# A Mixture-of-Experts layer on one core: how the weights of late expert blocks are loaded, and in which order those blocks run

## The reference

```python
lg = hf @ w_rg + b_rg                     # 8 groups
grp = argmax(lg)                          # top-1 group of a token
le_sel = (hf @ w_re + b_re) of that group # 8 experts in it
top_v, top_j = top_k(le_sel, 2)           # top-2 experts: 1024 choices, 64 experts
wts = softmax(lg)[grp] * softmax(top_v)
# each choice: (silu(x @ w_g[e]) * (x @ w_u[e])) @ w_d[e], weighted and added to its token
out = rmsnorm(x + sum of the two choices)
```

## Time and profile before

| | |
|---|---|
| time, median of 3 runs | 1350.87 us (1350.43 to 1354.53) |
| the profiled execution's own time | 1351.41 us |
| its span, first to last instruction | 1349.6 us |
| PE busy | 1156.8 us (86%) |
| DVE, ACT, POOL busy | 355.5, 234.3, 227.6 us |
| bytes moved by DMA | 435.80 MB, mean 323 GB/s |
| mean granted TensorE clock | 0.967 of full speed |
| chain that ended last | DMA 50%, PE 41%, DVE 4%, ACT 3% |

### The profile page before, as it was taken

How to read it: one execution, slowest core, us unless ns; L and a number is a source line. 1 busy time by engine, 2 the same in 40 slices (tenths; PEclk the granted TensorE clock), 3 DMA queues, 4 the chain that set the end, 5 groups by cost and what they waited for, 6 DMA issues and landing times.

```text
span 1349.6 us, 15238 instructions
## 1 busy us (share of the span) xinstructions
PE 1156.8 (86%) x5137; PEld 564.9 (42%) x5137; DVE 355.5 (26%) x700; ACT 234.3 (17%) x496; POOL 227.6 (17%) x271
## 2 busy tenths in 40 slices
PE   6999999999999999999888878777887778777881
PEld 5788777688843333333222222222222222222220
DVE  3899334444454222222000000000000000000004
ACT  4232324663100000000100000000001000010002
POOL 3455444083001000010010010000100010000100
PEclk9999999999999999999999999999999999999996
DMA  6431311314369999999999999999999999999974
GB/s 215 128 116 63 125 63 63 133 54 187 123 255 372 403 412 419 419 414 420 401 426 425 422 423 426 424 423 424 426 424 418 424 422 418 421 417 425 425 324 191
DMA packets 58516, 435.80 MB, mean 323 GB/s; under 512 B 10528, under 2 KB 10685, under 8 KB 26234
## 3 DMA queue, kind: packets, MB, share of 16 engines
q1 hardware_dynamic: 53034, 430.10, 77.4%
q0 software_dynamic: 5312, 5.28, 1.2%
q10 hardware_dynamic: 144, 0.07, 0.0%
HBM read 429.10 MB, written 18.36 MB: 332 GB/s over the span
## 4 chain that ended last, share of the span: by engine, by line
DMA 50%; PE 41%; DVE 4%; ACT 3%; issue 2%; SPq 1%; POOL 0%; POOLq 0%; DVEq 0%; ACTq 0%
DMA sb_weights<-in_w_exp_up 49%; PE ps_proj L1417 12%; PE ps_proj L1682 9%; PE ps_proj L1647 4%; PE ps_scores L1702 4%; PE ps_proj L1468 2%; PE ps_proj L1595 1%; PE ps_proj L1599 1%; PE ps_proj L1592 1%; PE ps_proj L1547 1%; PE ps_proj L1550 1%; PE ps_proj L1553 1%; DVE sb_x L1366 1%; PE ps_scores L1482 1%; PE ps_aT L1691 1%
## 5 line engine op out<-in xcount | busy, mean ns | idle before, releaser
L1682 PE MATMUL ps_proj<-sb_weights,sb_scratch 128*64 128x512 f32 x1984 | 471.7, 628 | 73.3 <-DMA sb_weights<-in_w_exp_up 71.9
L1682 PEld LDWEIGHTS ps_proj<-sb_weights,sb_scratch 128*64 128x64 f32 x1984 | 166.3, 144 | 371.8 <-issue 370.7
L1702 PE MATMUL ps_scores<-sb_weights,sb_scratch 128*64 128x512 f32 x992 | 228.5, 597 | 21.8 <-ACT sb_scratch L904 21.8
L1306 DVE TENSOR_TENSOR sb_scratch<-sb_scratch,ps_proj 128x256 f32<-128x256 f32 x62 | 26.1, 421 | 641.1 <-ACT sb_scratch L902 641.1
L659 POOL TENSOR_TENSOR sb_tick<-sb_tick 1x1 f32<-1x1 f32 x62 | 11.4, 184 | 882.5 <-ACT sb_scratch L909 783.4
L1702 PEld LDWEIGHTS ps_scores<-sb_weights,sb_scratch 128*64 128x64 f32 x992 | 67.0, 136 | 145.6 <-issue 109.5
L1417 PE MATMUL ps_proj<-sb_hT_r,sb_ring_r 128*128 128x512 f32 x512 | 124.0, 394 | 0.0
L902 ACT ACTIVATE sb_scratch<-ps_proj 128x256 f32<-128x256 f32 x62 | 23.8, 384 | 529.2 <-PE ps_proj L1682 529.2
L1417 PEld LDWEIGHTS ps_proj<-sb_hT_r,sb_ring_r 128*128 128x128 f32 x512 | 94.8, 188 | 26.9 <-issue 6.5
L604 POOL TENSOR_TENSOR sb_ring_r<-sb_ring,sb_ring_r 128x1024 fp32r<-128x1024 f32 x32 | 76.2, 2394 | 65.6 <-ACT sb_ring_r L721 64.6
L909 ACT ACTIVATE sb_scratch<-ps_scores 128x512 f32 (+1 forms) x62 | 37.0, 597 | 268.2 <-PE ps_scores L1702 268.2
(11 more groups left out here) (281 smaller groups left out, 872.1 us busy)
## 6 DMA issues: line engine op xcount, KB each, us to landing
sb_weights<-in_w_exp_up SPq DMA_DIRECT2D x62, 2048.0 KB, 14.9
sb_weights<-in_w_exp_down SPq DMA_DIRECT2D x62, 2048.0 KB, 10.5
sb_weights<-in_w_exp_gate SPq DMA_DIRECT2D x62, 2048.0 KB, 22.1
sb_ring<-in_w_in SPq DMA_DIRECT2D x9, 2048.0 KB, 9.0
sb_x<-in_x SPq DMA_DIRECT2D x8, 512.0 KB, 5.1
sb_dense<-expert_rows SPq DMA_DIRECT2D x4, 1024.0 KB, 7.9
sb_ring<-in_w_conv_pw SPq DMA_DIRECT2D x1, 2048.0 KB, 9.1
sb_ring<-in_w_attn_up SPq DMA_DIRECT2D x1, 2048.0 KB, 7.8
```

The source lines that it names most:

```text
L1306: dve.tensor_tensor(act, gsig, ps_gu[:, 256:512], ALU.mult).then_inc(act_ready, 1)
L1682: last = mm(ps_gu[g * BLK:(g + 1) * BLK, :].rearrange("p (a n) -> p a n", a=2), hTb[:, c, half * BLK:(half + 1) * BLK], weights[:, slice(6 ...
L1702: last = mm(ps_y[g * BLK:(g + 1) * BLK, :], actT[:, j, half * BLK:(half + 1) * BLK], weights[:, place(parity, 4 + half), 2 * j + g, :], st ...
```

## The change

Blocks 0 to 17 stay as they are: their weights are loaded one set for each block, in the order of the experts (`MINLOOP = 16` table places and the two first blocks). For the blocks behind them, the late ones:

- Late blocks of even experts take the even positions, in rising order of the expert; late blocks of odd experts take the odd positions, in falling order. A position is i, and its block is i + 2. Since even positions use the even weight set, all late blocks of one expert meet the same set, one after the other with a block of the other class between them.
- If one class has fewer blocks than the other, positions of that class at the end have no block; they run all the same, on rows that are scattered nowhere. The number of positions is 16 + 2 x the larger class.
- SP first runs its old loop for 16 places, then a second loop over loads: for load n it reads its position from `load_pos` and the expert from `expert_at`. A position whose expert was the expert of the position two before it has no load.
- PE reads for each late block from `load_at` how many loads must have landed: it waits for 16 * (loads + 1), where it waited for 16 * b.
- DVE reads for each late block from `nat_at` which place of the old order it is, and with that the offset and the row numbers: three reads of a register where one was.
- The tables are computed by DVE and PE: `late_turns` (eight instructions on at most 64 x 128 elements) and two instructions in `sorted_starts` (DVE), `turn_starts` and `turn_rows` (PE) in block 1, `list_turns` (DVE, eleven with its signal) behind `take_slots`, `load_row` (PE) and `list_loads` (DVE) ahead of block 16. Five new constants widen the table of constants from 1445 to 1881 columns of 512 bytes.
- ACT, POOL and PE wait for `turns_listed` in place of `listed`, and the special case of an odd count is gone.

With the reference's counts the late positions 16 to 59 hold, on the even side, experts 20, 22, 24, 26, 28, 30, 32, 34, 36, 38, 40, 42, 46, 48, 50, 52, 54, 56, 58, 60, 60, 62 (22 blocks), and on the odd side 63, 61, 61, 59, 59, 57, 55, 53, 51, 49, 47, 45, 43, 41, 39, 37, 35, 33, 27, 23, 21, 19 (22 blocks). So blocks 23, 27 and 58 have the expert of the block two before them.

The core of the diff:

```diff
 @@ SyncE
-            nblk = sp.value_load(count_i[0:1, 0:1], min_val=MINLOOP, max_val=MAXB - AHEAD)
-            with sp.Fori(0, nblk) as i:
-                e = sp.value_load(small_i[0:1, bass.ds(i, 1)], min_val=0, max_val=NE - 1)
+            def load_expert_weights(n, e, pos):
                 for third in range(3):
                     if third == 0:
-                        sp.wait_ge(gu_used, 2 * i + 2)
+                        sp.wait_ge(gu_used, 2 * pos + 2)
                     if third == 2:
-                        sp.wait_ge(down_used, i + 1)
-                    sp.wait_ge(in_w[third], 16 * i + 16)
+                        sp.wait_ge(down_used, pos + 1)
+                    sp.wait_ge(in_w[third], 16 * n + 16)
...
-                    load_third(i + AHEAD, third, bass.ds(e, 1), in_w)
+                    load_third(pos + AHEAD, third, bass.ds(e, 1), in_w)
+            with sp.Fori(0, MINLOOP) as i:
+                load_expert_weights(i, sp.value_load(small_i[0:1, bass.ds(i, 1)], min_val=0, max_val=NE - 1), i)
+            sp.wait_ge(turns_listed, 1)
...
+            sp.wait_ge(loads_listed, 1)
+            with sp.Fori(0, loads) as n:
+                pos = sp.value_load(load_pos[0:1, bass.ds(n, 1)], min_val=MINLOOP, max_val=MAXPOS - AHEAD)
+                e = sp.value_load(expert_at[0:1, bass.ds(pos, 1)], min_val=0, max_val=NE - 1)
+                load_expert_weights(n + MINLOOP, e, pos)
 @@ VectorE, in sorted_starts
+                link(dve.tensor_scalar(late_lo, efirst, float(MINLOOP), None, ALU.max))
+                dve.tensor_scalar(late_n, eend, float(MINLOOP), late_lo, ALU.max, ALU.subtract).then_inc(late_in, 1)
+            def late_turns():
+                dve.wait_ge(late_done, 1)
+                link(dve.tensor_copy(turn_lo, ps_oT[0:NE, 336:337]))
+                link(dve.tensor_tensor(turn_hi, turn_lo, late_n, ALU.add))
...
+                dve.tensor_scalar(late_b, ones_e, late_n, 1.0, ALU.mult, ALU.min).then_inc(loads_in, 1)
+            def list_turns():
+                dve.wait_ge(loads_done, 1)
...
+                dve.engine_nop().then_inc(turns_listed, 1)
+            def list_loads():
+                dve.wait_ge(loads_done, 2)
+                dve.tensor_scalar(load_pos[0:1, :], ps_oT[0:1, 344:344 + P], npos_f[0:1, :], None, ALU.min).then_inc(loads_listed, 1)
 @@ VectorE, late blocks
                 gate_and_up(i + AHEAD)
-                sorted_to_block(dve.value_load(start_i[0:1, 1:][:, bass.ds(i, 1)], min_val=0, max_val=2 * SEQ * KD))
-                list_rows(i + AHEAD, slots[:, AHEAD:][:, bass.ds(i, 1)])
+                nat = dve.value_load(nat_at[0:1, bass.ds(i + 1, 1)], min_val=0, max_val=MAXB - AHEAD - 1)
+                sorted_to_block(dve.value_load(start_i[0:1, bass.ds(nat, 1)], min_val=0, max_val=2 * SEQ * KD))
+                nat = dve.value_load(nat_at[0:1, bass.ds(i, 1)], min_val=0, max_val=MAXB - AHEAD - 1)
+                list_rows(i + AHEAD, slots[:, AHEAD:][:, bass.ds(nat, 1)])
 @@ TensorE
+            def turn_starts():
+                pe.wait_ge(late_in, 1)
+                mm(ps_oT[0:NE, 336:337], const("class_before", NE), late_n, start=True, stop=True)
+                mm(ps_oT[0:1, 338:340], late_n, const("class", NE), start=True, stop=True).then_inc(late_done, 1)
+            def turn_rows():
+                pe.wait_ge(loads_in, 1)
+                mm(ps_oT[0:1, 0:MAXPOS], const("expert", NE), hot_pos, start=True, stop=True)
+                mm(ps_oT[0:1, MAXPOS:2 * MAXPOS], nat_of, hot_pos, start=True, stop=True)
+                mm(ps_oT[:, 224:224 + MAXPOS], late_b, from_pos, start=True, stop=True).then_inc(loads_done, 1)
 @@ TensorE, late blocks
             def block_products(b, parity):
+                loads = pe.value_load(load_at[0:1, bass.ds(b - AHEAD, 1)], min_val=1, max_val=MAXPOS)
                 pe.wait_ge(hTb_ready, b + 1)
-                gate_up_half(b, parity, 0)
+                gate_up_half(b, parity, 0, loads)
```

109 lines of the change are left out of this document (79 added, 30 removed).

## The result

| | before | after |
|---|---|---|
| time, median of 6 runs | 1350.8 us (1350.4 to 1354.5) | 1320.5 us (1319.7 to 1321.8) |
| ratio, with its 95% interval | | 0.977 (0.976 to 0.978) |
| the profiled execution | 1351.41 us | 1319.66 us |
| its span | 1349.6 us | 1317.8 us |

The kernel became faster by 30.3 us. I had said 20.9 us, in a range of 1320 to 1342: the direction and the mechanism of the skipped loads hold, the size does not. The profile shows the same difference (31.8 us in the span), so it can be taken apart there.

What follows compares the result with a forecast made beforehand. Late blocks were taken to be bound by weight loads. Skips -24.4, tables +2.4, late-block entry +0.5 and constants +0.6 gave -20.9 us, so 1330.0 us, in a range of 1320 to 1342.

Steps and rivals of the forecast that it cites:

- What bounds the kernel: Blocks 20 to 61: loads set the pace at 15.11 us, against PE's 12.44; before block 16 PE sets it.
- rival (A): Whole kernel: the forecast itself, three loads skipped and time 1325 to 1336 us; chance 0.58.
- The gap at a skip: Load behind a skipped one: restart takes 13.96 us, DMA loses 6.4 us, so a skip gains 8.7 us.
- Rival (B): Loads behind skips: cheaper restart, 12.8 us, gaps 5.3, 5.3 and 7.0, gain 27.7 us, time 1323 to 1327; chance 0.15.
- The pace of the loads: Late blocks bound by loads: one load takes 15.11 us, held unchanged by the sum.
- rival (C): Late loads: new expert order changes the pace by 0.2 us a load, 8 us either way, 1322 or 1338; chance 0.10.
- Block 26 is then waited for again, at 51.8: Between the first two skips: block 26's weights land 51.8 us after block 22 starts, so the DMA limits again.
- The last skip: Block 58: counted with the low clock ahead of it, gap 8.1 us, gain 7.0 us.
- the sign that the gaps are smaller than I say: Block 61's start: over 26 us earlier would mean smaller gaps; about 21 us was expected.
- The tables: Ahead of block 16: DVE's instructions delay PE 1.5 us in block 1, `turn_rows` 0.9, the late-block entry 0.5.
- my 0.6 us: Start of kernel: the 218 KB of added constants land later and cost 0.6 us, from 0 to 1.
- The register reads: Late-block loop: PE's read of 0.5 us a block has 3 us of cover, costing nothing; uncovered, 6 us.

Runs made afterwards that it cites:

- four_apart: Changed kernel with a load at every late position except four, eight positions apart (blocks 26, 34, 42, 50): 1320.6 us.
- after_wider_constants: Changed kernel with 112 unused columns more in the table of constants (1993): 1324.8 us.
- all_loads: Changed kernel with a load for every late position, none skipped, constants 1993 columns wide: 1357.3 us, ratio 1.004 to the kernel before.
- halves: Changed kernel with gate and up loaded in four 1 MB transfers, the first two issued after half 0 of the products: 1309.1 us, ratio 0.969.
- halves_tables_moved: As halves, with the late-block count ahead of block 0's gating product and `late_turns` where DVE waits for `start_rows`: 1308.4 us, ratio 0.9675.
- both_upwards: Changed kernel with odd experts in rising order too, so skips fall on blocks 55, 58 and 59: 1330.3 us, ratio 0.984.
- before_halves: Kernel before with gate and up loaded in four 1 MB transfers, nothing skipped: 1351.5 us, ratio 1.000.

## Why the prediction was wrong in size

By its own steps:

- **What bounds the kernel** was right: late blocks waited for up thirds, and every load not made was time won. So was rival (A) in its mechanism, with 59 loads and blocks 24, 25, 28, 29, 59 and 60 without a wait.
- **The gap at a skip** was the first step that failed. I said that "the queue run dry" costs what block 18 showed, 13.96 us. That row was read without asking what else was in the queue: it was still delivering at 389 GB/s when the load was issued, and an instruction packet fell into the load. Measured: 12.6 us from gate's issue to up's landing, gap 5.1 us (5.2 in four_apart). after_wider_constants isolates it, with the old pace and no low clock ahead of a skip: against all_loads its three skips are worth 30.4 us (blocks 22 to 30 and 57 to 61), where I had 26.1 for this case. The 4.3 us more are 3 x 1.4 us. Rival (B) had 12.8 and 5.3, from the 7.8 us of a load of 2 MB alone, at a chance of 0.15. Its price for the skips, 27.7 us, is within 2 us of the measured 29.5.
- **The pace of the loads** was the second, and the larger. My sum held it at 15.11 us and had only costed the extra bytes of the constants; it was 14.95. I had a change of pace as rival (C), for a wrong reason. The experts' order does nothing to it (all_loads). The wider table of constants moved the weights onto a boundary of 256 bytes: 4.9 us in the stretches without a skip, 0.16 us a load, and the reverse in after_wider_constants.
- **"Block 26 is then waited for again, at 51.8"** needed both to fail. With 12.6 us and my pace its weights would come at 50.4, PE at 49.8. They landed at 771.01, 49.5 us after block 22's start, since the loads behind the restart came 14.7 us apart; block 26 started at 49.8. So eight blocks in a row ran at PE's pace, and a smaller gap would bring nothing more between these two skips unless PE can run ahead for longer, as in halves.
- **The last skip** has the low clock ahead of it, as I had counted (block 57, 8.78 us), and gave 9.0 us for 7.0: the restart is 1.4 us cheaper, and the rest is pace, here and in the kernel before.
- **In all**, an estimate from these figures, 4 of the 10.9 us that the span is off belong to the restart, 6 to the pace, 0.7 to the part ahead of block 16. Block 61 started 31.7 us earlier; I had named over 26 as the sign that the gaps are smaller than I say, and that sign could not tell the gaps from the pace.
- **The tables** cost more than the 2.8 us by which block 16 starts later. The first gating product of DVE, before and after:

```profile
394.19 0.42 DVE L1306 TENSOR_TENSOR sb_scratch<-sb_scratch,ps_proj 128x256 f32<-128x256 f32 x1 [2.60 <-ACT sb_scratch L902]
```

```profile
393.57 0.42 DVE L1376 TENSOR_TENSOR sb_scratch<-sb_scratch,ps_proj 128x256 f32<-128x256 f32 x1 [2.60 <-ACT sb_scratch L936]
```

  From it to block 16 the kernel before takes 243.6 us, the changed one 247.0: 3.4 us, of which 1.7 arise up to block 1's gating product, 0.9 in `turn_rows` and 0.8 at the entry to the late blocks. I had 1.5, 0.9 and 0.5. What the wider constants cost ahead of this the spread of 3.4 us in the start of the expert phase hides; my 0.6 us is neither shown nor refuted. In block 1, DVE's eight instructions run one after the other:

```profile
403.82 0.15 DVE L1276 COPY sb_work<-ps_oT 64x1 f32<-64x1 f32 x1 [0.16 <-PE ps_oT L1751]
...
405.65 0.28 DVE L1284 TENSOR_SCALAR sb_work<-sb_consts,sb_work 64x128 f32<-64x128 f32 x1
...
410.84 0.41 DVE L1376 TENSOR_TENSOR sb_scratch<-sb_scratch,ps_proj 128x256 f32<-128x256 f32 x1
```

and PE waits for the gating product (L1376, the old L1306):

```profile
411.31 0.51 PE L1784 MATMUL ps_aT<-sb_consts,sb_scratch 128*128 128x128 f32 x2 [1.43 <-DVE sb_scratch L1376]
...
416.80 0.35 PE L1756 MATMUL ps_oT<-sb_work,sb_consts 64*1 64x112 f32 x2
...
417.27 0.47 PE L1758 MATMUL ps_oT<-sb_work 64*128 64x112 f32 x2
```

  The eight end at 405.93, so the estimate of 1.9 us held (2.1), and so did the 0.9 us of `turn_rows` (416.80 to 417.68). halves_tables_moved gets 1.5 us of this back.
- **The register reads** in the loop are hidden as I said: blocks with their weights there follow at 12.44 us, as before.
- The time is at the lower edge of the range, because two errors of one sign met: (B) and (C) together, which I had weighed only one by one. That it did not fall below is luck.

## What to carry to other kernels

Take the price of a restart only from a place where the queue was empty and nothing else large moved during the load: read the DMA's speed ahead of the issue and the list of queues over the load. Where a kernel is bound by its loads, see where their destination begins in a partition, since any buffer declared ahead moves it; a multiple of 256 bytes was worth 1% of the load time, 4 to 5 us here. A transfer left out is worth its time less the gap until the next may be issued, as long as the consumer can run ahead, so skips should lie apart. A smaller unit of buffering gave 5.7 us at the skips and 4.4 us in the full stream, and nothing there when its transfers became slower off the boundary. And before the starts of two executions are compared, both are to be counted from a point behind which they run alike: ahead of the expert phase they differ by up to 3.4 us here, behind it an edit of 1.5 us can be read.

## What the runs showed of the hardware that I had not expected

- Loads of 2 MB into 128 partitions ran at 427 to 428 GB/s from 860 to 1190 us where the destination begins at a multiple of 256 bytes in each partition, and at 422 to 425 GB/s where it does not (64, 128, 288 and 448 bytes behind one of 512).
- Two transfers of 1 MB in place of one of 2 MB cost 0.17 us a block of 6 MB off such a boundary (15.28 against 15.11) and 0.09 on it (15.04 against 14.95).
- From 860 to 1190 us the granted clock was 0.95 of full speed in the kernel before. One wait of 2.4 to 2.5 us comes there ahead of 12 of the 22 blocks and one of 0.7 to 1.0 us ahead of the others, and the products of 9 took 8.8 us in place of 7.1. In before_halves each block has two waits, of about 1.0 and 1.3 us, and the clock was 1.00 in the same stretch, though PE waited longer in all (84.8 us against 68.6 between 637 and 1280). It saved no time there, as the loads are the bound.
- An empty queue delivered the second of two loads of 2 MB 12.0 us after its issue at all three skips of the changed kernel. With one packet of 16 KB of the instruction queue in the load it was 13.1 us in both_upwards.
